# Pooling and triangular inversion in one interleaved stage, on 128 partitions in three batches

## What is computed

```python
def box_mean_grid(u, window, rows):          # u: four groups of 128 channels, windows 2, 4, 8, 16
    ...                                      # mean over a centred window of the grid, clipped at the edges
    return (s / cnt).reshape(B, T, C).astype(u.dtype) - u

def pool_branch(u, mean_fn, w_pool, pool_scale, w_b_out):
    outs = [jnp.einsum('btc,cd->btd', mean_fn(u[..., j * POOL_GROUP:(j + 1) * POOL_GROUP], win), w_pool[j])
            for j, win in enumerate(POOL_WINDOWS)]
    return (jnp.concatenate(outs, axis=-1) * pool_scale) @ w_b_out

    gates = jax.nn.sigmoid(z[..., SHIFT_COLS + D_B:] + b_gate)
    m = gates[..., :D_MODEL] * ya + gates[..., D_MODEL:] * yb

def rwkv_step(S, inp):                       # the recurrence
    r, w, k, v, a, b = inp
    sa = jnp.einsum('bdhvk,bdhk->bdhv', S, a)
    S = S * w[..., None, :] + sa[..., None] * b[..., None, :] + v[..., None] * k[..., None, :]
    return S, jnp.einsum('bdhvk,bdhk->bdhv', S, r)
```

## Time and profile before

| | us |
|---|---|
| median of 3 runs | 2484.5 (2482.86 to 2487.03) |
| the profiled execution, its own time | 2488.41 |
| its span in the profile | 2486.7 |
| busy: PE, DVE, ACT, POOL | 2014.3, 1677.6, 883.3, 679.8 |
| mean granted clock of TensorE | 0.913 |
| projection ends, `pools` begins | 364.2 |
| `invert` begins | 432.4 |
| `scan` begins (its first transfer is issued) | 674.4 |
| PEER | from 1100 to the end |

### The profile page before, as it was taken

How to read it: one execution, slowest core, us unless ns; L and a number is a source line. 1 busy time by engine, 2 the same in 40 slices (tenths; PEclk the granted TensorE clock), 3 DMA queues, 4 the chain that set the end, 5 groups by cost and what they waited for, 6 DMA issues and landing times.

```text
span 2486.7 us, 37653 instructions
## 1 busy us (share of the span) xinstructions
PE 2014.3 (81%) x14541; PEld 1226.6 (49%) x14541; DVE 1677.6 (67%) x3588; ACT 883.3 (36%) x1823; POOL 679.8 (27%) x593
## 2 busy tenths in 40 slices
PE   5999948778688899788999887778877777778777
PEld 3876626657577776575555432333333333333333
DVE  4599975489135454658777687777777777777764
ACT  4566642454545553323222312121222121212221
POOL 0000011000022221003444345444444445444441
PEclk7999979989589999999999998988888989888998
DMA  6477652823344431629999999999999999999995
GB/s 241 136 243 246 232 214 81 269 70 137 118 182 152 155 137 46 220 102 374 421 420 421 421 378 421 420 420 420 420 421 420 420 420 421 419 421 421 421 421 225
DMA packets 146147, 742.74 MB, mean 299 GB/s; under 512 B 17680, under 2 KB 37040, under 8 KB 77360
## 3 DMA queue, kind: packets, MB, share of 16 engines
q0 software_dynamic: 73728, 536.90, 52.0%
q1 hardware_dynamic: 71088, 201.33, 22.7%
q10 hardware_dynamic: 1152, 2.10, 0.2%
HBM read 684.58 MB, written 55.69 MB: 298 GB/s over the span
## 4 chain that ended last, share of the span: by engine, by line
DMA 30%; PE 15%; DVE 4%; issue 3%; ACT 2%; POOL 1%; DVEq 0%; ACTq 0%
DMA uv<-in_uv_in,ic 24%; PE bank L2750 13%; DMA uvx<-in_uv_in,ic 6%; DVE xt L2644 1%; POOL uv L2474 1%; ACT dg L2554 1%; PE bank L92 1%; PE bank L94 1%; PE bank L93 1%; POOL uvx L2474 0%; PE bank L2730 0%; ACT ge L2549 0%; ACT L2549 0%; ACT L2392 0%; DVE wql L2605 0%
## 5 line engine op out<-in xcount | busy, mean ns | idle before, releaser
L2750 PE MATMUL bank<-uv,dg 128*128 128x512 f32 x1664 | 817.4, 649 | 198.2 <-ACT dg L2554 197.7
L2474 POOL DMA_INDIRECT uv<-in_uv_in,ic x416 | 472.3, 1135 | 735.7 <-PE bank L2750 567.0
L2750 PEld LDWEIGHTS bank<-uv,dg 128*128 128x128 f32 x1664 | 337.2, 208 | 665.9 <-issue 404.6
L2644 DVE SCALAR_TENSOR_TENSOR qt_<-uv,gr 128x1024 f32<-128x1024 f32 x288 | 352.8, 1225 | 158.3 <-DMA uv<-in_uv_in,ic 141.7
L2549 ACT ACTIVATE ge<-dt_ 128x4 f32<-128x4 f32 (+1 forms) x130 | 26.7, 205 | 938.0 <-DVE qt_ L2644 744.7
L2750 PE MATMUL bank<-uvx,dg 128*128 128x512 f32 x384 | 186.2, 642 | 47.6 <-ACT dg L2554 47.2
L2644 DVE SCALAR_TENSOR_TENSOR xt<-uv,gr 128x1024 f32<-128x1024 f32 x128 | 156.9, 1226 | 45.9 <-DMA uv<-in_uv_in,ic 36.7
L2554 ACT ACTIVATE dg<-ident,gc_ 128x128 f32<-128x128 f32 x512 | 163.9, 390 | 30.9 <-DVE gc_ L2649 29.3
L2644 DVE SCALAR_TENSOR_TENSOR qt_<-uvx,gr 128x1024 f32<-128x1024 f32 x96 | 117.6, 1225 | 58.4 <-DMA uvx<-in_uv_in,ic 55.6
L2750 PEld LDWEIGHTS bank<-uvx,dg 128*128 128x128 f32 x384 | 76.7, 205 | 157.0 <-issue 90.4
L2474 POOL DMA_INDIRECT uvx<-in_uv_in,ic x96 | 118.0, 1229 | 115.2 <-PE bank L2750 103.6
(11 more groups left out here) (363 smaller groups left out, 3694.7 us busy)
## 6 DMA issues: line engine op xcount, KB each, us to landing
wt<-in_wrow_in SPq DMA_DIRECT2D x32, 512.0 KB, 4.8
wraw<-in_wpair_in SPq DMA_DIRECT2D x24, 512.0 KB, 3.6
pair_record<-rec SPq DMA_DIRECT2D x16, 768.0 KB, 5.2
pair_record<-rec SPq DMA_DIRECT2D x8, 1536.0 KB, 7.0
xb<-pair_record SPq DMA_DIRECT2D x16, 768.0 KB, 7.4
lkb<-pair_record SPq DMA_DIRECT2D x8, 1536.0 KB, 8.6
lvar<-pair_record SPq DMA_DIRECT2D x16, 768.0 KB, 8.4
wraw<-in_wq_in SPq DMA_DIRECT2D x18, 512.0 KB, 7.8
```

The lines of the kernel that those rows point to most:

```text
L2474: pool.indirect_dma_start(ring(i), None, g["uv_in"], bass.IndirectOffsetOnAxis(ap=ic[:, s % ICR, k:k + 1], axis=0)).then_inc(su[row_slot[i ...
L2644: dve.scalar_tensor_tensor(junk, ring(i)[:, 0:D], 1.0, hc[:, t % 2, :], ALU.mult, ALU.mult, accum_out=dt[:, k:k + 1]).then_inc(s_ud, 1)
L2750: mm = pe.matmul(acc(t, c)[:, :], dg[:, n % 2, k, :], ring(i)[:, D + 512 * c:D + 512 * c + 512], start=h == 0 and q == 0 and k == 0, stop= ...
```

## The change

- **Pool inputs in the projection.** Four weight tiles follow the projection's own on the same buffers: SP loads them between the last record stores, ACT has four more `high`, DVE four more `low`, PE `pool_input(0..3)` of 24 split matmuls each: two ahead of the last `bonus`, two behind it, ahead of the transpose of `colv`. They stay in PSUM banks 2, 3, 0, 1.
- **One stage `middle`** in the place of `pools` and `invert`. Pooling is interleaved with the first five pairs' products and eight gate pieces. Its scratch lies in the unused third of `ts` and in `gt`, `gz`, `xy`. `yb_dram` is gone: `branch(j)` makes one branch at a time in bank 5, and `gated(j)` reads it there. The branch weights come in eight loads of 256 KB instead of one of 2 MB.
- **Three batches of 64 units.** The 192 units are NBAT = 3 batches of NU = 64; the first heads of the 64 units lie on partitions 0 to 63, the second heads on 64 to 127, each with its two diagonal blocks in the free dimension: 128 partitions with 2 blocks in place of 96 with 4. Each transposed group is 16 transposes of 64 x 64 (8 columns for each half): the lower half as a transpose, the upper half as a matmul against the identity, in turn, into the same bank. A group is copied by one or two ACT instructions of 128 x 512 columns in place of 384.
- `gz` and `gt` have two buffers. In the last batch DVE does half of the copies of the corners and those of `xt_out`. A batch has four rounds of `inner` and four of `corner`, 24 in all as before.
- `x_dram` is stored batch by batch in pieces cut at pair borders (3, 4 and 3); ACT's first copy into `xb` of batches 1 and 2 waits until the stores of the batch before have landed (as `turned_out(1)` did before).
- GpSimd clears three padded grids ahead of the constants; before, it cleared eight in `pools`.

```diff
-            pools(nc, sb, sem, locals())
-            invert(nc, sb, sem, locals())
+            middle(nc, sb, sem, locals())
...
+    POOLED = ((2, 1), (3, 1), (0, 0), (1, 0))
...
-                    src = g["wlora_in"] if j is None else g["wpair_in"][j]
-                    q = i if j is None else ORDER[i]
+                    src = g["wlora_in"] if j is None else g["wpair_in"][j] if j < NPAIR else g["wz_in"][NW - 1 - (n - NT)]
+                    q = i if j is None else ORDER[i] if j < NPAIR else 0
...
+                high(NT + 2)
                 exps(NPAIR - 1)
+                high(NT + 3)
...
+                    if j == NPAIR:
+                        low(NT + 2)
                     dot(4 * j + 1)
...
                         keys_out(j - 1)
+                    if j == NPAIR:
+                        low(NT + 3)
...
+                def pool_input(i):
+                    n, (b, back) = NT + i, POOLED[i]
+                    pe.wait_ge(s_lo, n + 1)
+                    pe.wait_ge(s_zs, NT - back)
+                    hi, lo = tokens[1]
+                    for k in range(KT):
+                        mm = split_mm(pe, bank[b][:, :], wh[:, n % 2, k, :], wl[:, n % 2, k, :], hi[:, k, :], lo[:, k, :],
+                                      k == 0, k == KT - 1)
                     mm.then_inc(s_z, 1)
...
+                pool_input(0)
+                pool_input(1)
                 pe.wait_ge(s_at, 4 * NPAIR)
                 bonus(NPAIR - 1)
+                pool_input(2)
+                pool_input(3)
                 pe.wait_ge(s_cv, 1)
...
+    TAKEN = (2, 3, 0, 1)
+    ZB, YB = (6, 7), 5
+    PARTS = ((2, 0, 8, 0), (3, 0, 8, 1), (4, 8, 4, 0), (5, 8, 4, 1))
...
+                for a in (uu[0], uu[1], cr):
+                    pool.memset(a, 0.0).then_inc(s_z0, 1)
+                done(pool.memset(hf[:, :], 0.5))
...
+                    for j, a, e in PIECES[b]:
+                        if b < NBAT - 1:
+                            sp.wait_ge(s_zc, 8 * b + 8)
+                        else:
+                            sp.wait_ge(s_zc, 8 * b + (e - 1 - NU * b) // 16 + 1)
+                            sp.wait_ge(s_zd, (e - 1 - NU * b) // 16 + 1)
+                        sp.dma_start(x_dram[j, :, (a - NPU * j) * CHUNK:(e - NPU * j) * CHUNK],
...
+                branch(7)
+                weights(22, 23)
+                gated(4)
+                weights(24, 25, 26)
                 stored(1)
-                sp.wait_ge(s_xs, 16 * NPAIR)
+                weights(27)
+                gated(5)
+                weights(28, 29)
+                stored(2)
+                gated(6)
+                weights(30, 31)
+                gated(7)
...
+                def x_out(b, n):
+                    if b and n == 0:
+                        act.wait_ge(s_xs, SAVED[b])
+                    act.wait_ge(s_rx, 4 * b + n + 1)
+                    for k in range(2):
+                        act.activation(xb[:, 0:NU, HB * k + 8 * n:HB * k + 8 * n + 8].rearrange("p u t -> p t u"),
+                                       bank[n % 2][:, :].rearrange("p (t u) -> p t u", t=8), ACT.Copy,
+                                       scale=mb[:, k:k + 1]).then_inc(s_rxc, 1)
...
+                branch_high(7)
+                gate(22)
+                corner(1, 0, 1)
+                gate(23)
+                corner(1, 2, 3)
+                x_out(2, 0)
+                x_out(2, 1)
+                gate(24)
+                x_out(2, 2)
+                x_out(2, 3)
+                inner(2, 0, 1)
+                gate(25)
+                inner(2, 2, 3)
+                corner(2, 0, 1, 2, 3)
+                for m in range(26, NZ):
                     gate(m)
-                turned_out(1)
-                for r in range(6):
-                    inner(1, r)
-                for r in range(6):
-                    corner(1, r)
...
                 def gated(j):
+                    dve.wait_ge(s_yb, j + 1)
                     dve.wait_ge(s_gk, 2 * j + 2)
-                    dve.wait_ge(s_yl[j % 2], 16 * (j // 2) + 16)
-                    dve.scalar_tensor_tensor(yb[:, j % 2, :], tb[:, j % 2, :], 1.0, yb[:, j % 2, :], ALU.add, ALU.mult).then_inc(s_gb, 1)
+                    if j >= 2:
+                        dve.wait_ge(s_bs[j % 2], 16 * (j // 2))
+                    dve.scalar_tensor_tensor(yo[:, j % 2, :], tb[:, j % 2, :], 1.0, bank[YB][:, :], ALU.add, ALU.mult).then_inc(s_gb, 1)
...
+                    ch(dve.tensor_copy(z[:, :, :, :], eye[:, :, :].unsqueeze(1).broadcast_to((P, 2, HB, HB))))
+                    dve.wait_ge(s_ric, 8 * b + 8)
...
+                        ch(dve.tensor_tensor(o, z[:, :, 0:n, u:u + 1].broadcast_to((P, 2, n, w)),
+                                             t[:, :, u:u + 1, n:HB].broadcast_to((P, 2, n, w)), ALU.mult))
+                        ch(dve.tensor_tensor(z[:, :, 0:n, n:HB], z[:, :, 0:n, n:HB], o, ALU.add))
+                        between(u)
+                    dve.sem_inc(s_inv, 1)
+                    dve.tensor_copy(gy[b % 2], z[:, :, :, :].rearrange("p k s t -> p s k t")).then_inc(s_gy, 1)
...
+                def third(u):
+                    if u in (4, 9, 18, 22, 26, 30):
+                        low({4: 19, 9: 20, 18: 21, 22: 22, 26: 23, 30: 24}[u])
+                    if u == 1:
+                        gated(3)
+                        branch_low(5)
+                    if u == 15:
+                        gated(4)
+                        branch_low(6)
...
+                substituted(0, first)
+                substituted(1, second)
+                substituted(2, third)
+                low(25)
+                for n in range(4):
+                    dve.wait_ge(s_rt, 8 + n + 1)
+                    dve.tensor_copy(xy[:, :, 8 * n:8 * n + 8].rearrange("p u s -> p s u"),
+                                    bank[2 + n % 3][:, :].rearrange("p (s u) -> p s u", s=8)).then_inc(s_rtd, 1)
+                gated(5)
...
+                gated(6)
+                low(29)
+                low(30)
+                low(31)
+                gated(7)
...
+                def turned(p, out, block):
+                    if p:
+                        return pe.matmul(out, block, ident[half(1), half(1)], start=True, stop=True)
+                    return pe.transpose(out, block, ident[half(0), half(0)])
...
+                def branch(j):
+                    if j == 0:
+                        pe.wait_ge(s_tc, 4 * NPAIR)
+                        pe.wait_ge(s_plo, NW)
+                    else:
+                        pe.wait_ge(s_gb, j)
+                    pe.wait_ge(s_bl, j + 1)
+                    for i, q in enumerate(ORDER):
+                        mm = split_mm(pe, bank[YB][:, :], wbh[:, j % 2, q, :], wbl[:, j % 2, q, :], p_hi[:, q, :], p_lo[:, q, :],
+                                      i == 0, i == NW - 1)
+                    mm.then_inc(s_yb, 1)
...
+                    for n in range(8):
+                        if b < 2 and 8 * b + n >= 2 or n >= 2:
+                            pe.wait_ge(s_ric, 8 * b + n - 1)
+                        for i in range(8):
+                            for p in range(2):
+                                mm = turned(p, bank[n % 2][half(p), 64 * i:64 * i + 64], ts[half(p), NU * b:NU * b + NU, 8 * n + i])
+                        mm.then_inc(s_ri, 1)
...
+                gate(22)
+                corner(1, 0, 1)
+                gate(23)
+                corner(1, 2, 3)
+                x_out(2, 0)
+                x_out(2, 1)
+                gate(24)
+                x_out(2, 2)
+                x_out(2, 3)
+                xt_out(2)
+                inner(2, 0, 1)
+                gate(25)
+                inner(2, 2, 3)
+                corner(2, 0, 1, 2, 3)
+                branch(6)
+                gate(26)
+                gate(27)
+                gate(28)
+                branch(7)
+                for m in range(29, NZ):
                     gate(m)
-                turned_out(1)
-                for r in range(6):
-                    inner(1, r)
-                for r in range(6):
-                    corner(1, r)
```

More of the change, by code:

```diff
@@ L1280, in _ @@
                 act.wait_ge(s_hb, 1)
[L1281 to L1293 removed]
+                gate(0)
@@ new lines, in _ @@
+                products(5)
+                gate(8)
+                products(6)
+                gate(9)
+                products(7)
+                branch(0)
+                gate(10)
+                turned_in(1)
+                gate(11)
+                branch(1)
+                gate(12)
+                gate(13)
+                x_out(0, 0)
+                x_out(0, 1)
+                gate(14)
+                x_out(0, 2)
+                x_out(0, 3)
+                xt_out(0)
+                turned_in(2)
@@ L1474, in _ @@
[L1474 to L1480 removed]
+                x_out(1, 0)
+                x_out(1, 1)
+                gate(19)
+                x_out(1, 2)
+                x_out(1, 3)
```

(5 more changed lines are left out.)

791 lines of the change are left out of this document (388 added, 403 removed).

## The result

The changed kernel takes 2656.1 us (median of 4, 2653.97 to 2662.03), the kernel before 2485.77 (2482.86 to 2489.91): the medians are 1.0685 apart, and the comparison of all the runs gives 1.0698 (95% interval 1.0685 to 1.0711). It is 170 us slower where I had forecast 25 us faster, and far outside my range.

What follows compares the result with a forecast made beforehand. DVE was taken to bound the substitution, PE and ACT the two ends. Head 72, substitution 143 and tail 62.5 give -30.2 us, with the projection's +5 -25.2: 2460 us, forecast 2452 to 2470, 8 in 10 2442 to 2483.

Steps and rivals of the forecast that it cites:

- the price of a transposed group: In turning in and out: 16 transposes of 64 x 64 at 58 ns each take 0.92 us a group.
- Rival 1: In the transposed groups: row halves take turns, 114 ns an instruction, a group 1.8 us, 2493 us in all; chance 0.10.
- rival 2: In the middle stage: waits between engines eat most of the gain, leaving -15 there, 2477 us in all; chance 0.18.
- The clock: On PE before the first substitution step: slow clock adds 1.4 us.
- The substitution term: From first to last substitution step: 143 us in place of 149.7, of which 16 are new waits.
- The head: From the projection's end to the first substitution step: 72 us in place of 112.3, bounds 64 and 80.
- The tail: After the last substitution step: 62.5 us in place of 45.7, bounds 54 and 75.
- the wait for the stores: In the tail: ACT's first copy of `x_out(2)` waits until `stored(1)` has landed; 5.5 us of it shows.
- The sum: From the projection's end to `scan`: head, substitution and tail together, 278 to 282 us.
- The projection's +5: At the projection's end: 96 added split matmuls and four more `low` cost 5 us, bounds +2.5 and +9.

Runs made afterwards that it cites:

- transposes as cheap as I had assumed: Changed kernel with all identity products as matmuls reading neighbouring elements; turned_in takes other elements, ACT's copy scaled by zero, so not the layer: 2470.8 us, one execution.
- the best such run with 64 x 64 turns that can be had: Changed kernel with all turns as matmuls, contiguous `x_out`, and batch 1's results in a second buffer: 2475.71 us, 0.9970 of the kernel before.
- early inputs alone: Kernel before with only the pool inputs made at the projection's end, two stages and two batches of 96 kept: 2473.14 us, 0.9963 of the kernel before.

## Why the prediction was wrong

- **The step that failed is the price of a transposed group**, 0.92 us. I took it from the 64 x 64 matmuls of the earlier trace rows and wrote that no row shows a transpose beside a matmul. That row differs from the new instructions in two ways, and both cost: it has no change of operation (with it, 0.28 us an instruction in place of 0.058), and it reads neighbours (without them, 0.113). With 768 such instructions on TensorE each 0.01 us is 7.7 us of its time.
- **My bounds did not cover it.** I bounded the unknown above by twice the row, because the only mechanism I had looked for was that the halves take turns. The mixture of two operations stood in the code, and I named it ("for a transpose beside a matmul no row here speaks at all") without pricing it. Rival 1 had the right place and the right sign and was too low: at 114 ns it gives +8, the truth was 280 ns and +170. Its cause, that the halves take turns in the common bank, is what the runs refute: a pair costs 0.67 us at half clock in one half as in two.
- **What the extra time on TensorE does** I had seen in rival 2 as a few microseconds: `gated(j)` waits for `branch(j)`, and the steps stand behind it. With TensorE as the bound this wait is 101 us in two places.
- **The clock.** 40 us of nothing but pairs ran at 0.50. I had 1.4 us for slow clock in the head. The pairs with a transpose are not needed for it: all matmuls grouped by half ran at 0.50 as well, from 434 to 456 us, with TensorE busy 22 of 22 us.
- **The substitution term is right**, and not by luck: with transposes as cheap as I had assumed, 142.7 against 143, DVE's two waits 9.9 and 6.9 us against 16, a step of 62 columns 0.22 and one of 512 columns 0.68, by 0.15 + 1.04 ns a column 0.21 and 0.68.
- **The head** is 80 in that run and not 72. TensorE begins 9.7 us after the stage (9.8), but is then busy 52 us where I had 41.2 with the slow clock in it; the granted clock was 0.80 up to 434 us and 0.76 behind that. **The tail** is 72 and not 65 (62.5 and the 2.5 to `scan`), where the wait for the stores is 9.2 and not 5.5; the other 3.6 us I have not traced. The sum would have been 294 and not 280.
- **The projection's +5 was near.** In the ten kernels with the early inputs it is 2.5 to 3.5 us longer, counted from its own first transfer; the changed kernel begins the next stage earlier than the kernel before (361.61 against 364.21) only because its projection began 5.8 us earlier. The rows' store comes 5.4 to 7.0 us later in the projection, for which I had 4.3, and the next stage begins 3.0 to 4.3 us behind it in place of 6.5, which I had not in the sum. From the first pair's `tbo` to the last one's it is 2.3 us more, about the two `low` of 1.23. The clock was better than I feared: 0.93 from 331 to 346 us where it had been 0.68 with TensorE idle, and from 347 us on the two inputs behind `bonus` are 0.23 us a matmul.
- **Had the transposes cost what I took**, the whole would have been 2470.8 in one execution against 2483.67 (-13), half of my -25. The stretches give the same: 16 us less in the stage and 3.3 more in the projection. Whether the zeros in that kernel do anything to the clock, no run shows. So the reasoning on the merged stage was right in direction and optimistic by half. The part that gains for sure, 10.5 us, is the pool inputs' move. Merging and three batches together then bring 15 us in the head, lose 5 in the substitution and 16 in the tail, where eight gate pieces and two branches now stand behind the last step: 301 in the best such run with 64 x 64 turns that can be had, 296 with early inputs alone.

## What to carry to other kernels

Price an instruction by a row that has its operation, its neighbours on the queue and its access pattern; if there is none, take as its bound what such instructions last from start to end (here 0.27 us for the transpose and 0.43 for the matmul, 0.70 a pair where 0.56 was measured), and not a multiple of the spacing of a pipelined row. Do not mix 64 x 64 transposes with matmuls on TensorE one by one: turn a block with a matmul against the identity where the other half must be one, and let the halves take turns. And count how many instructions hang on a price before trusting it: 768 times 0.2 us was six times all that the change could bring.

## What the runs showed of the hardware

- A float32 64 x 64 matmul against the identity, with the two row halves in turn at full clock: 60 to 62 ns each with neighbouring elements, 113 to 118 with a stride of 32 or 64 elements in the stationary operand. When eight of one half follow one another: 175 to 193, with a stride or without. The halves in turn write one bank and are the faster order.
- Eight 64 x 64 transposes in a row: 75 ns each at full clock. A transpose and a matmul in turn: 560 ns a pair at full clock, 670 at half, in one row half as in two.
- In 40 us in which TensorE was busy throughout with such pairs its granted clock was 0.50; so it was over 22 us of nothing but matmuls grouped by half.
